# Empty buffers that shift weights, operands and inner tensors of a hybrid decoder step within a 128 byte line

## The reference

```python
x = x + 0.5 * _swiglu(_rmsnorm(x, g_ffn1), w1_gate, w1_up, w1_down)   # 2048 -> 5504 -> 2048
h = _rmsnorm(x, g_mix)
proj = h @ w_in                                                        # 2048 -> 7192
# 8 heads of forgetting attention (prompt, and sample with a paged cache of 256 rows),
# 8 heads of mLSTM (prompt in a chunked form, sample from a state C, n, m)
y = concatenate([y_a, y_m]) @ w_out                                    # 2048 -> 2048
x = x + y
x = x + 0.5 * _swiglu(_rmsnorm(x, g_ffn2), w2_gate, w2_up, w2_down)

def _swiglu(x, w_gate, w_up, w_down):
    return (silu(x @ w_gate) * (x @ w_up)) @ w_down
```

## Time and profile before

| | before |
|---|---|
| time, median of 3 runs | 2404.87 us (2399.09 to 2404.95) |
| the profiled execution | 2404.53 us |
| its span, first to last instruction | 2402.9 us |
| PE / PEld busy | 97% / 94% |
| DVE / ACT / POOL busy | 51% / 35% / 2% |
| DMA engines, mean busy share | about one half |
| mean granted TensorE clock | 0.98 of full |

### The profile page before, as it was taken

How to read it: one execution, slowest core, us unless ns; L and a number is a source line. 1 busy time by engine, 2 the same in 40 slices (tenths; PEclk the granted TensorE clock), 3 DMA queues, 4 the chain that set the end, 5 groups by cost and what they waited for, 6 DMA issues and landing times.

```text
span 2402.9 us, 47905 instructions
## 1 busy us (share of the span) xinstructions
PE 2337.7 (97%) x17725; PEld 2270.2 (94%) x17725; DVE 1220.0 (51%) x1869; ACT 841.9 (35%) x1098; POOL 48.6 (2%) x81
## 2 busy tenths in 40 slices
PE   7999999999999999998899989999999999999998
PEld 6999999999999999876899959999999999999998
DVE  6555454444454464554357764564555344555443
ACT  4333333333333443332234433343333233333332
POOL 2000000000000010000000110000000000000000
PEclk9999999999999999988999988999999999999999
DMA  5555555555554444446355543455555555555553
GB/s 159 177 163 160 168 161 175 164 169 161 169 159 167 166 146 139 164 162 207 109 170 158 154 123 105 148 177 166 158 169 162 163 169 175 158 168 162 164 168 127
DMA packets 175661, 383.91 MB, mean 160 GB/s; under 512 B 18949, under 2 KB 44669, under 8 KB 175245
## 3 DMA queue, kind: packets, MB, share of 16 engines
q1 hardware_dynamic: 172736, 375.98, 49.5%
q0 software_dynamic: 2432, 5.57, 0.8%
q10 hardware_dynamic: 416, 1.32, 0.2%
HBM read 373.09 MB, written 9.70 MB: 159 GB/s over the span
## 4 chain that ended last, share of the span: by engine, by line
PE 94%; DVE 4%; ACT 1%; DMA 1%; issue 1%; SPq 0%; ACTq 0%; POOL 0%; DVEq 0%; POOLq 0%
PE ps L1539 29%; PE ps L1541 29%; PE ps L1540 29%; DVE w_lo L896 1%; PE ps L1768 1%; PE ps L1627 1%; PE ps L1781 0%; PE ps L1590 0%; DVE C L1456 0%; DVE w_raw L1456 0%; PE ps L1739 0%; DMA x_rows<-in_x_sample 0%; DVE xt L922 0%; ACT w_hi L571 0%; DVE sq L913 0%
## 5 line engine op out<-in xcount | busy, mean ns | idle before, releaser
L896 DVE TENSOR_TENSOR w_lo<-w_raw,w_hi 128x1024 fp32r<-128x1024 f32 (+1 forms) x690 | 788.4, 1184 | 1041.6 <-ACT w_hi L571 1041.6
L571 ACT CAST w_hi<-w_raw 128x1024 fp32r<-128x1024 f32 (+1 forms) x690 | 669.1, 1017 | 1329.1 <-PE ps L1541 1326.3
L1539 PE MATMUL ps<-x_hi,w_hi 128*128 128x288 f32 (+1 forms) x2752 | 816.4, 297 | 5.0 <-DVE w_lo L896 3.2
L1540 PE MATMUL ps<-x_lo,w_hi 128*128 128x288 f32 (+1 forms) x2752 | 812.7, 295 | 0.0
L1541 PE MATMUL ps<-x_hi,w_lo 128*128 128x288 f32 (+1 forms) x2752 | 810.0, 294 | 0.0
L1539 PEld LDWEIGHTS ps<-x_hi,w_hi 128*128 128x128 f32 x2752 | 516.5, 188 | 6.0 <-DVE w_lo L896 3.3
L1541 PEld LDWEIGHTS ps<-x_hi,w_lo 128*128 128x128 f32 x2752 | 519.2, 189 | 0.0
L1540 PEld LDWEIGHTS ps<-x_lo,w_hi 128*128 128x128 f32 x2752 | 517.5, 188 | 0.1
L1539 PE MATMUL ps<-hid_hi,w_hi 128*128 (+1 forms) x1376 | 407.1, 296 | 1.5 <-DVE X L1071 1.5
L1540 PE MATMUL ps<-hid_lo,w_hi 128*128 (+1 forms) x1376 | 406.9, 296 | 0.0
L1541 PE MATMUL ps<-hid_hi,w_lo 128*128 (+1 forms) x1376 | 406.8, 296 | 0.0
(11 more groups left out here) (440 smaller groups left out, 1363.9 us busy)
## 6 DMA issues: line engine op xcount, KB each, us to landing
w_raw<-in_w_down SPq DMA_DIRECT2D x178, 512.0 KB
w_raw<-in_w_gate SPq DMA_DIRECT2D x320, 256.0 KB
w_raw<-in_w_up SPq DMA_DIRECT2D x320, 256.0 KB
w_raw<-in_w_in SPq DMA_DIRECT2D x64, 512.0 KB
w_raw<-in_w_in SPq DMA_DIRECT2D x64, 384.0 KB
w_raw<-in_w_out SPq DMA_DIRECT2D x32, 512.0 KB
page<-in_cache_k SPq DMA_DIRECT2D x16, 512.0 KB, 3.6
w_raw<-in_w_gate SPq DMA_DIRECT2D x32, 192.0 KB
```

Source lines behind the costliest of these rows:

```text
L571: nc.scalar.copy(w_hi[:, slot, 0:width], w_raw[:, slot, 0:width]).then_inc(w_hi_ready, 1)
L896: nc.vector.tensor_tensor(w_lo[:, slot, 0:width], w_raw[:, slot, 0:width], w_hi[:, slot, 0:width].bitcast(F32), ALU.subtract).then_inc(w_l ...
L1539: mm(out, hi, x_hi[:, k, :], start=first and pair == 0 and s == slots[0], stop=False)
L1540: mm(out, hi, x_lo[:, k, :], start=False, stop=False)
```

## The change

Three kinds of tensors are added that nothing reads or writes. No instruction is added, taken away or moved.

```diff
     pages_sb = t_("pages_sb", [1, NB * NPG], I32)
+    t_("w_offset", [P, 8])
     X = t_("X", [P, KD, T])
     w_raw = t_("w_raw", [P, SLOTS, UW])
...
     def swiglu_memory(n):
         scope, l_ = area("left")
         with scope:
+            if n == 1:
+                l_("x1_offset", [P, 16])
             x = x0 if n == 0 else (l_("x1_hi", [P, KD, T], F32R), l_("x1_lo", [P, KD, T], F32R))
+            l_(f"hid_offset{n}", [P, 8 if n == 0 else 8])
             return dict(x=x, hid=(l_(f"hid_hi{n}", [P, CHUNK, T], F32R), l_(f"hid_lo{n}", [P, CHUNK, T], F32R)),
                         gate=l_(f"gate{n}", [P, 4, T]), up=l_(f"up{n}", [P, 4, T]))
```

## The result

| | before | changed |
|---|---|---|
| time, median of 9 runs each | 2404.95 us (2396.53 to 2413.62) | 2386.06 us (2382.67 to 2397.26) |
| ratio, 95% interval | | 0.9921 (0.9903 to 0.9939) |
| ratio, measured a second time (a2, 6 runs) | | 0.9939 (0.9914 to 0.9963) |
| span of the profiled execution | 2402.9 us | 2384.4 us |
| mean granted clock in it | 0.980 | 0.983 |

The account below looks back on a forecast made before the run. PE was taken as the bound, with 15,840 products at 133.3 ns each. From 2404.5 us, 29 us (1.8 ns a product) came off, splits, DMA and the rest at 0: 2375.5, given as 2376; 8-in-10 range 2340 to 2430.

Parts of the forecast that it names:

- The bound and the excess: PE sets the time; 15,840 products at 133.3 ns, 13.3 ns each above the array's 120, 211 us in all.
- The half clock: Sign to check: products at the lower granted clock, 1.2 GHz, must stay at 240 ns; some 30 such products in all.
- the splits: Splitting w_raw and x into hi and lo: distances or durations cost nothing, means stay at 1017 and 1184 ns.
- The price of distance: Nonzero distance between operands of all 15,840 products saves 1.8 ns each, 29 us; bounds 0, -13.3 and +2.7 ns.
- the gates: First neighbour: same xm, 288 columns, 24-column weight blocks mostly not at distance 0; 131.5 ns, 1.8 less than 133.3.
- The second neighbour: mLSTM score stage, 256 columns at distances 96 and 64: 125 ns against 106.7, excess 18 ns; speaks against the change.
- The third neighbour: Products just after a PE hold-up: 134 ns, then 130, later 133.3; so pace depends on how streams stand together.
- The rule of the Trainium skill: A second read port serves TensorE weight loads; by it distance means nothing and time stays at 2404.5 us.
- One price for all distances: The same -1.8 ns was put on every product group, whether its new distance was 96, 32 or 64.
- Nothing happens: Rival: the 13.3 ns is a cost of each fp32r product, distance doesn't enter; 2404 us (2397 to 2412), chance 0.31.
- Slower: Rival: distance 0 is the good one; products at 136 ns, +2.7 each, 2447 us, or 2426 for half; chance 0.17.
- Much faster: Rival: the excess goes, each product at 120 ns, 2193 us, or 2349 or about 2300 in part; chance 0.10.

Follow-up runs that it names:

- m1: Benchmark in place of the layer: bare product stream, 384 matmuls in each of 31 cases of start addresses; 288-column full-weight cases took between 131.1 and 135.4 ns a product.
- e5: Changed kernel with other buffer sizes: x0, xm, y and x1 at distance 32, hid0 and hid1 at 0; ratio 1.0006 to before.
- e7: The program of e5 run once more unchanged, a single run for its trace; x1's second stage at 133.3 ns, y at 134.4; no total time given.
- e6: Changed kernel with hid0 and hid1 at distance 64 in place of 32 and 96; ratio 0.9943 to before.
- m2: Same bare-stream benchmark as m1 with 55 other cases of addresses and column counts; no 288-column case went below 131.1 ns.
- e2: Changed kernel with another 128 bytes between hi and lo of x1, hid0 and hid1; ratio 0.9938 to before.

## Why the prediction came out as it did

**The bound and the excess: right.** PE set the time, one product cost 133.3 ns of which 13.3 are not the array's, and the change acted on that and on nothing else. The half clock stayed at 240 ns (21 matmuls in 5 us after), and the splits at 1017 and 1185 ns. Two readings beside it were off without any weight in the sum: PE's longest wait before was 10.1 us, on line 1590 for DVE, not some 5, and the trace of before has 47 products at the half clock, not some 30.

```profile
PE ps L1590 <- DVE sq_r L927: 10.1, 1, 10.1
```

**The price of distance: right in sign, by a reason that was wrong.** The prediction took -1.8 ns from the gates and put it on all 15,840 products: 29 us, 2376. Measured were -1.11 ns on 11,712 and 0 on 4128: 13 us. That is the step that failed, the size of the term. The gates' blocks of 24 weight columns are enough for their gain: the benchmark has 131.11 ns for such blocks at distance 0, as fast as any, and 131.77 and 131.67 at 32 and 64, between which the gates' 131.5 lies. So that row said nothing in favour of a distance. The prediction had this as a bound ("0, if the gates' 1.8 ns come from their short weights alone") and should have taken it for the likelier reading: it knew two differences and gave the whole to one.

**The second neighbour: read from too little.** The 125 ns of the earlier trace rows came from one head and from starts rounded to 10 ns. Over the eight heads, the product on `b_row_r` in that place takes 116 to 122 ns to the next start, 119.4 on average, an excess of 12.7 over the array's 106.7. In a stream by themselves 256 columns take 117.8 ns, an excess of 11.1, at distance 0 and at 64 (m1). Neither is more than the 13.3 of 288 columns, so the row bore on nothing, against the change or for it.

**The third neighbour: the right mechanism.** That the pace is a pattern of streams and not a constant of the instruction is what m1, e5 and e7 show directly.

**The rule of the Trainium skill** (SBUF, "A bandwidth-pool intuition that's wrong", and TensorE: Matmul & The Clock Gate, Part 2, step 1), that loading the next tile's weights takes no read bandwidth from the running matmul, would leave the place of the weights without effect. Here it has one, of 1.7%: in m1 the columns and their addresses stay the same while w_lo moves by 32 bytes, and the pace goes from 133.33 to 131.11 ns. No run shows whether what is lost is read bandwidth or something else.

**One price for all distances: wrong.** Distances 96, 32 and 64 were treated alike. hid, whose lo lies 207 lines behind hi, gained nothing at 32 or at 96, and would have at 64 (e6). The prediction also named its own test of the idea: stages of the same distance should show the same count. x0, xm, y and hid1 all stand at 96, and hid1 stayed at 133.33 ns while the others went to 132.2. Distance modulo 128 by itself is therefore not what sets the pace.

**The rivals.** "Nothing happens" was true for the hid stages. "Slower" is real as a mechanism: 134.4 ns at distance 32 with the x offset, 135.4 at 4 bytes. In the changed kernel no operand shows it (hid0, at 32, stays at 133.3), and its price was put too high (136 ns in all products). "Much faster" had nothing for it, and no case of 288 columns came below 131.1.

**Why the median was as near as 10 us.** The term was 16 us too large, and the runs of the first measurement had the upper clock for longer than those of before, which returned 6 us of it. That part is luck: at like clock the change is worth 13 us where the forecast had 29.

**What stays open.** The runs show that the pace depends on the places of four streams, in lines and within a line. No rule was found that tells the pace of a layout, each case of the benchmark was traced once (the two that stand in both m1 and m2 agree), and which accesses meet in the memory was not measured. Nor is it known what the 11 ns are that were left in every case, beyond that they grow with the columns, and that at the lower clock a product takes no more than its 240 ns.

## What to carry to other kernels

When one engine is busy from end to end, compare the distance between two starts with the engine's own pace; here 13 of 133 ns were hidden in a profile that said 97% busy. Placement in memory can be worth a per cent or two in such a stream, but the best place can't be argued from one number such as the distance modulo 128. A small benchmark of the bare stream over many start addresses found in two launches a layout worth 2.6 times as much as the change (33.7 against 13 us), and its paces carried over to the kernel to 0.1 ns, except at distance 32, where two paces exist. With effects below 1%, put the granted clock of each run beside its time before comparing medians.

## What the runs showed of the hardware that was not expected

- The pace of a stream of fp32r matmuls settles in most cases at one of a few sharp values, 0.56 or 1.11 ns apart: 131.11, 131.67, 132.22, 132.78, 133.33 and 134.44 ns for 288 columns (a few cases, such as 132.60, 132.96 and 135.42, lie elsewhere). The single steps from start to start within such a pattern still vary between 125 and 144 ns.
- Shifting the second of two weight tensors by 32 or 96 bytes gave 2.2 ns for each product with the x offset (with the hid offset 1.1 and 2.2), against 1.7 ns for the best distance of the moving operand (16 bytes) and 1.1 ns for those of the change.
- The full clock gives less than twice the half clock: 240.0 ns for 288 columns at 1.2 GHz, never under 131.1 at 2.4 GHz.
- At some addresses two steady paces exist (133.3 and 134.4 ns at distance 32, in e2, e5 and e7), each held to the end of its stretch, up to 268 us.
- The time of this kernel moves with its mean granted clock by 2.07 us for each 0.001, and that clock differed between 0.977 and 0.986 from run to run.
